# Latent attention: the products with the values one unit later and between the scores and the transposes

## The chip, the cores and the metric

The kernel runs on one core of one Trainium2 chip. The metric is the time of one execution on the device in microseconds (us), lower is better. TensorE is the matrix engine, ScalarE, VectorE and GpSimd (POOL in the profile) are the other compute engines, SyncE (SP) issues the DMAs.

## The reference

Two sequences of 1024 tokens, width 1024, go through two layers of an encoder. Every layer normalises x, projects it with `w_in` to the columns of four head groups, and mixes them: a short gated convolution (A), multi-head latent attention (B), a Conformer convolution (C) and windowed attention (D). The four results are gated, joined, multiplied by `w_out`, normalised and added to x. What the change touches is group B:

```python
def attend(args):
    qn_b, qr_b = args
    sc = (jnp.einsum('bqhd,bkhd->bhqk', qn_b, k_nope)
          + jnp.einsum('bqhr,bkr->bhqk', qr_b, k_rot)).astype(jnp.float32) * scale
    p = jax.nn.softmax(sc, axis=-1).astype(v.dtype)
    return jnp.einsum('bhqk,bkhd->bqhd', p, v)
```

There are 4 heads of 64 value columns, and a query has 64 + 32 rotary columns. Every query sees all 1024 keys.

## The kernel before, in words

The program makes four passes, one for each layer of each sequence. Each engine has its own instruction list, written out by hand in one block per engine, and runs it strictly in order; semaphores connect them. The numbers are fp32 split into a high and a low fp32r part, so that a product is three matmuls (high x high, high x low, low x high).

A pass is: input projection (L535, with the windowed attention worked into it), the latent up-projections (L696 to L720), the attention loop of group B, and the output product (L814). The attention loop works on **units**. A unit u is one head (u // 8) and one block of 128 queries (u % 8), 32 units in all (`NB`). Two units make a pair w = u // 2, whose 256 queries go through the products with the values together. A unit needs:

- **S(u)**, `b_scores`, TensorE L763: six matmuls of 512 columns, the scores of 128 queries against 1024 keys, into one of two pairs of PSUM banks. It waits until the exponential of unit u-2 has read that pair (`be_ok`).
- the **max** of each row, `b_max`, VectorE L1613, and the **exponential** with its sum, `b_exp`, ScalarE L1211, into `Pb`.
- **T(u)**, `b_transpose`, TensorE L778: eight transposes of 128x128, in two halves, into banks 4 and 5. It waits for the exponential of u (`be_ok`) and until VectorE is done with the same half of unit u-1 (`bpt_lo`).
- the **high part**, `b_hi`, ScalarE L1219, and the **low part**, `b_lo`, VectorE L1349, two instructions each, from PSUM into `PTb`.
- **V(u)**, `b_out`, TensorE L798: eight matmuls of 256 columns. V(2w) takes the first four blocks of 128 keys of pair w, V(2w+1) the other four. Both write columns 0 to 255 of bank 6 + w % 2. In front of V(2w) stands **R(w)**, TensorE L793, two transposes that spread the reciprocals of the sums over columns 256 to 511 of the same bank. R(w) waits for the reciprocals (`br_ok`), and until the combine of pair w-2 has read the bank (`bo_ok`). V(2w) then waits for all low parts of the pair.
- the **tmpB copy**, `b_half`, ScalarE L1230, and the **combine**, `b_combine`, VectorE L1634, L1635 and L1637: the two parts added, times gate, times reciprocal, into `cat`. The combine signals `bo_ok`.

The order is that of the loops over i, one on each engine. In step i TensorE issues S(i), T(i-1) and V(i-3). VectorE issues the max of i, the low parts of i-1, and in even steps from 6 on the combine of pair (i-6)/2 (with the reciprocals of a pair in between). ScalarE issues the high parts of i-1, the exponential of i, and in odd steps from 5 on the tmpB copy of pair (i-5)/2. ScalarE also does other work there: in steps 10, 11, 18 and 19 it copies keys and queries of the heads 2 and 3 (`HEAD_AT`), in steps 20, 22, 24, 26 and 28 it splits a block of `w_out` (`W_OUT_AT`, L1041), and in 27, 31 and 32 it splits columns of `cat` for the output product, whose first two blocks TensorE issues in step 33. The wait that R(w) makes, and the end of the combine, are these lines:

```python
if half == 0:
    if w >= 2:
        pe.wait_ge(*got("bo_ok", w - 1))
...
own.add(tt(b[rows, 0:256], b[rows, 0:256], t, ALU.add))
own.add(stt(y_, b[rows, 256:512], 0.5, y_, ALU.mult, ALU.mult))
own.wait()
tt(y_, b[rows, 0:256], y_, ALU.mult).then_inc(q["bo_ok"], 1)
```

Of the kernel before, what the change touches and what calls it, by code (L numbers as in the profile page):

```python
# [88 lines left out]
NB = HEADS * NT  # L89
# [34 lines left out]
def build(nc, x, w_in, w_out, w_q, w_kv, w_pw, par, g_pre, g_post, rel_bias, onehot, band, rope, y):  # L124
    with ExitStack() as ctx:
# [190 lines left out]
        def got(name, n, ahead=0):  # L316

            return q[name], (now[0] + ahead) * TOTAL[name] + n
# [60 lines left out]
        with nc.Block() as block:  # L379
# [128 lines left out]
            def _(pe):  # L508
                pe.wait_ge(p_id, 2)
                for p in range(PASSES):  # L510
# [218 lines left out]
                    def pointwise(m):  # L729
                        dst = (bank67, bank45)[m]  # L730
                        if m == 0:
                            pe.wait_ge(*got("clo_ok", 2))
                            pe.wait_ge(*got("bc_cp", 2))
                        else:
                            pe.wait_ge(*got("y_ok", 2))
                        for j in range(2):
                            for a, b in three:
                                z = (cHi, cLo)[b]
                                for h in range(2):
                                    last = mm(dst[:, h * HALF:(h + 1) * HALF], wpR[:, a, j, m * P:(m + 1) * P],  # L740
                                              z[:, j, h * HALF:(h + 1) * HALF],
                                              start=(j == 0 and (a, b) == (0, 0)),
                                              stop=(j == 1 and (a, b) == (1, 0)))
                        last.then_inc(q["pw_mm"], 1)
# [23 lines left out]
                    def b_transpose(u):  # L768

                        pe.wait_ge(*got("be_ok", u + 1))  # L770
                        for half in range(2):
                            if u >= 1:
                                pe.wait_ge(*got("bpt_lo", 2 * u + half - 1))
                            else:
                                pe.wait_ge(*got("pw_ok", 2))
                            for k in range(NT // 2):
                                col = half * HALF + k * P
                                last = tr(ps[:, 4 + half, k * P:(k + 1) * P], Pb[:, u % 2, col:col + P], ident[:, :])  # L778
                            last.then_inc(q["bt_mm"], 1)

                    def b_out(w, half):


                        h = 2 * w // NT
                        bank = ps[:, 6 + w % 2, :]
# [3 lines that stand above are left out]
                            elif w == 0:  # L789
                                pe.wait_ge(*got("pw_ok", 1))  # L790
                            pe.wait_ge(*got("br_ok", w + 1))
                            for i in range(2):
                                tr(bank[:, 256 + i * P:256 + (i + 1) * P],  # L793
                                   brc[:, 2 * w + i:2 * w + i + 1].broadcast_to([P, P]), ident[:, :])
                            pe.wait_ge(*got("bpt_lo", 4 * w + 4))
                        for k in range(half * NT // 2, (half + 1) * NT // 2):
                            for part in range(2):
                                last = mm(bank[:, 0:256], Vb[:, k, h, :, :], PTb[:, w % 2, part, k, :],  # L798
                                          start=(k == 0 and part == 0), stop=(k == NT - 1 and part == 1))
                        if half:  # L800
                            last.then_inc(q["bo_mm"], 1)
# [18 lines left out]

                    pe.wait_ge(*got("vb_lo", NT))
                    pointwise(0)
                    for i in range(NB + 3):
                        if i == 1:
                            pointwise(1)
                        if i < NB:
                            b_scores(i)
                        if 1 <= i < NB:
                            b_transpose(i - 1)
                        if i == NB + 1:  # L830
                            out_product(0, (0, 1))
                        if i >= 3:
                            b_out(*divmod(i - 3, 2))
                        if i == NB:
                            b_transpose(NB - 1)


                    out_product(0, range(2, KD))
# [136 lines left out]
            def _(act):  # L975
# [33 lines left out]
                for p in range(PASSES):  # L1009
# [192 lines left out]
                    def q_hi(h):  # L1202
                        Q, rows = ((Qe, slice(0, HD)), (Qo, slice(HD, P)))[h % 2]
                        act.wait_ge(*got("ch_done", C["bqn0"] + 1))
                        act.activation(Q[rows, 0, :], (chunk_ps("bqn0"), qF2)[h // 2][rows, :], ACT.Copy).then_inc(q["q_hi"], 1)
# [7 lines left out]
                    def b_hi(u):  # L1213
                        w = u // 2
                        if w >= 2:
                            act.wait_ge(*got("bo_mm", w - 1))
                        for half in range(2):
                            act.wait_ge(*got("bt_mm", 2 * u + half + 1))
                            act.activation(PTb[:, w % 2, 0, half * NT // 2:(half + 1) * NT // 2, u % 2 * P:(u % 2 + 1) * P],  # L1219
                                           ps[:, 4 + half, :].rearrange("p (k t) -> p k t", t=P), ACT.Copy  # L1220
                                           ).then_inc(q["bpt_hi"], 1)

                    def b_half(w):
                        h = 2 * w // NT
                        act.wait_ge(*got("bo_mm", w + 1))
                        if w >= 2:
                            act.wait_ge(*got("bo_ok", w - 1))
                        r, o = ((0, HD), (HD, 0))[h % 2]
                        b = ps[:, 6 + w % 2, :]
                        act.activation(tmpB[r:r + HD, w % 2, :], b[o:o + HD, 0:256], ACT.Copy).then_inc(q["bo_tmp"], 1)  # L1230
# [8 lines left out]
                    k_hi(1)  # L1239
                    q_hi(0)  # L1240
                    q_hi(1)
                    for i in range(NB + 4):
                        if i in HEAD_AT:
                            h = HEAD_AT[i]
                            (q_hi if i % 2 else k_hi)(h)
                        if 1 <= i <= NB:
                            b_hi(i - 1)
                        if i < NB:
                            b_exp(i)
                        if i >= 5 and i % 2 == 1:  # L1250
                            b_half((i - 5) // 2)
                        if i in W_OUT_AT:
                            split_hi(f"w_out{W_OUT_AT[i]}")
                        if i == CAT_A_AT:
                            act.wait_ge(*got("bs_mm", NB - NT))
                            cat_hi(0, slice(0, 2))
                        if i in (NB - 1, NB):
                            act.wait_ge(*got("bo_ok", NB // 2 - NT // 2 + 1))
                            cat_hi(i - NB + 1, slice(2, KD) if i < NB else slice(0, KD))
# [40 lines left out]
            def _(dve):  # L1300
# [41 lines left out]
                for p in range(PASSES):  # L1342
# [284 lines left out]
                    def b_combine(w):  # L1627
                        h, i = divmod(2 * w, NT)
                        dve.wait_ge(*got("bo_tmp", w + 1))
                        r = HD * (h % 2)  # L1630
                        rows = slice(r, r + HD)
                        b, t = ps[:, 6 + w % 2, :], tmpB[rows, w % 2, :]
                        y_ = cat[rows, 2 + h // 2, i * P:(i + 2) * P]
# [4 lines that stand above are left out]
# [7 lines left out]
                    k_lo(1)  # L1645
                    q_lo(0)
                    q_lo(1)
                    for i in range(NB + 5):
                        if i < NB:
                            b_max(i)  # L1650
                        if i == 0:
                            pointwise_gate(0)
                            pointwise_gate(1)
                        if 1 <= i <= NB:
                            if i % 2 == 0:
                                b_recip(i // 2 - 1)
                            b_lo(i - 1)
                        if i >= 6 and i % 2 == 0:
                            b_combine((i - 6) // 2)

                    for k in range(EARLY, KD):
                        split_lo(f"w_out{k}")
# [136 lines left out]
```

## Time and profile before

| what | value |
|---|---|
| median of 3 runs | 2217.1 us (2217.02 to 2217.55) |
| profiled execution, its own time | 2217.08 us |
| profiled execution, span from first to last instruction | 2215.2 us |
| granted TensorE clock, mean | 0.999 |
| busy: TensorE matmuls, weight loads, VectorE, ScalarE, GpSimd | 98%, 83%, 73%, 44%, 25% |

In the profile PE is TensorE, PEld its weight loads, DVE VectorE, ACT ScalarE and POOL GpSimd. A row of the timeline names its start, how long the merged instructions took, the engine, the source line, what is written and read, and how many instructions it merges; the number in brackets is the engine's idle time in front of it and who ended it. Matmuls overlap in their pipeline: the duration of a group runs past the start of the next group, so the step from start to start is the time it occupies.

### The profile page before, as it was taken

What the parts mean: (1) busy time and instruction counts of PE and PEld (TensorE: products, weight loads), DVE (VectorE), ACT (ScalarE), POOL (GpSimd) and SP (SyncE); (2) the same over time, 40 slices, a digit from 0 to 9 for tenths busy, and PEclk for the clock granted to TensorE, in tenths of its full rate; (3) what the DMA queues carried; (4) which work ended last, traced back from release to release, by engine and by line L of the source; (5) the groups of instructions that cost most, each with busy time, mean ns of one, the idle gap of its engine ahead of it and who ended that gap; (6) DMA issues with size and microseconds to landing.
All of it is one profiled execution on the core that took longest, in us unless ns stands there. A gap on an engine that the chain in (4) does not pass through costs nothing.

```text
span 2215.2 us, 29044 instructions
## 1 busy us (share of the span) xinstructions
PE 2178.0 (98%) x11394; PEld 1834.1 (83%) x11394; DVE 1616.2 (73%) x2050; ACT 982.5 (44%) x1731; POOL 545.4 (25%) x316
## 2 busy tenths in 40 slices
PE   7999999999999999999999999999999999999998
PEld 7888887888888888788888888878888888887887
DVE  5499877975459987896455998789654699878853
ACT  4333335863333433585333343368533334337841
POOL 2122223221122232232111233223211212323310
PEclk9999999999999999999999999999999999999999
DMA  5111111034111111103311111100432111110012
GB/s 182 58 39 52 31 42 49 10 113 146 67 66 39 43 39 43 39 19 146 113 61 63 39 43 39 53 29 23 154 111 76 39 48 43 39 43 29 30 67 95
DMA packets 38951, 136.34 MB, mean 62 GB/s; under 512 B 4736, under 2 KB 5248, under 8 KB 38816
## 3 DMA queue, kind: packets, MB, share of 16 engines
q1 hardware_dynamic: 38816, 134.47, 18.0%
q8 instruction: 93, 1.52, 0.3%
q14 instruction: 42, 0.34, 0.1%
HBM read 116.63 MB, written 17.83 MB: 61 GB/s over the span
## 4 chain that ended last, share of the span: by engine, by line
PE 91%; DVE 5%; ACT 2%; issue 1%; DMA 0%; SPq 0%; DVEq 0%; ACTq 0%
PE ps L535 48%; PE ps L814 14%; PE ps L763 7%; PE ps L798 5%; PE ps L778 5%; PE ps L640 2%; PE ps L614 2%; PE ps L628 2%; DVE accC L1430 2%; PE ps L696 1%; PE ps L283 1%; PE ps L740 1%; PE ps L545 1%; DVE woR L1349 1%; PE ps L793 1%
## 5 line engine op out<-in xcount | busy, mean ns | idle before, releaser
L535 PE MATMUL ps<-hT,stat 128*128 128x512 f32 x4416 | 1055.1, 393 | 0.8 <-DVE Qst L1349 0.8
L535 PEld LDWEIGHTS ps<-hT,stat 128*128 128x128 f32 x4416 | 816.6, 188 | 164.1 <-issue 2.9
L890 POOL TENSOR_TENSOR stat<-raw,stat 128x1024 fp32r<-128x1024 f32 x92 | 250.1, 2719 | 871.2 <-ACT stat L1041 871.2
L1430 DVE SCALAR_TENSOR_TENSOR accC<-uC,parT,accC 128x1024 f32<-128x1024 f32 x240 | 421.4, 1793 | 2.6
L814 PE MATMUL ps<-woR,catR 128*128 128x512 f32 x1488 | 343.7, 391 | 3.4 <-DVE woR L1349 3.4
L814 PEld LDWEIGHTS ps<-woR,catR 128*128 128x128 f32 x1488 | 277.6, 188 | 61.9 <-DVE woR L1349 5.1
L1613 DVE TENSOR_REDUCE bnb<-ps 128x1 f32<-128x1024 f32 x128 | 156.2, 1220 | 43.1 <-PE ps L763 42.4
L1219 ACT ACTIVATE PTb<-ps 128x512 fp32r<-128x512 f32 x256 | 139.0, 595 | 81.0 <-PE ps L778 78.8
L1349 DVE TENSOR_TENSOR PTb<-ps,PTb 128x512 fp32r<-128x512 f32 x256 | 163.4, 679 | 12.8 <-ACT PTb L1219 11.9
L1211 ACT ACTIVATE Pb<-ps,bnb 128x1024 f32<-128x1024 f32 x128 | 143.0, 1118 | 21.0 <-DVE bnb L1613 20.0
L798 PE MATMUL ps<-PTb,Vb 128*128 128x256 f32 x1024 | 151.4, 292 | 0.0
L778 PEld LDWEIGHTS ps<-ident,Pb 128*128 128x128 f32 x1024 | 117.7, 140 | 28.1 <-ACT Pb L1211 13.2
L778 PE MATMUL ps<-ident,Pb 128*128 128x128 f32 x1024 | 133.7, 273 | 5.5 <-ACT Pb L1211 5.0
L1289 ACT ACTIVATE junk<-ps 128x1024 f32<-128x1024 f32 x31 | 31.8, 1027 | 236.7 <-PE ps L814 236.7
L1108 ACT ACTIVATE PTd<-ps 128x768 fp32r<-128x768 f32 (+1 forms) x64 | 48.6, 759 | 189.5 <-PE ps L628 189.5
L798 PEld LDWEIGHTS ps<-PTb,Vb 128*128 128x128 f32 x1024 | 129.5, 190 | 0.0
L1693 DVE TENSOR_SCALAR oss<-oss 128x1 f32<-128x1 f32 x31 | 4.8, 154 | 156.5 <-ACT junk L1289 134.8
L1115 ACT ACTIVATE tmpD<-ps 64x128 f32<-64x128 f32 x64 | 17.5, 273 | 207.4 <-PE ps L640 207.4
L1047 ACT ACTIVATE th<-ps 128x1024 f32<-128x1024 f32 x40 | 41.1, 1027 | 144.0 <-PE ps L535 144.0
L763 PE MATMUL ps<-Ke,Qe 96*128 96x512 f32 x384 | 100.1, 396 | 0.0
L1453 DVE CUSTOM_DVE_ANT_0 Pd<-ps,bias,ngs 128x384 f32<-128x384 f32 (+1 forms) x128 | 67.2, 563 | 44.8 <-PE ps L614 44.8
L763 PE MATMUL ps<-Ko,Qo 128*128 128x512 f32 x384 | 99.6, 394 | 0.0
(201 smaller groups left out, 2809.9 us busy)
## 6 DMA issues: line engine op xcount, KB each, us to landing
raw<-w_in SPq DMA_DIRECT2D x100, 512.0 KB, 3.5
y<-xs SPq DMA_DIRECT2D x31, 512.0 KB, 2.6
raw<-w_out SPq DMA_DIRECT2D x24, 512.0 KB, 3.6
xs<-x SPq DMA_DIRECT2D x16, 512.0 KB, 3.6
xs<-y SPq DMA_DIRECT2D x16, 512.0 KB, 3.5
xd<-x SPq DMA_DIRECT2D x8, 512.0 KB, 9.0
ropeT<-rope SPq DMA_DIRECT2D x4, 1024.0 KB, 5.7
rawX<-w_out SPq DMA_DIRECT2D x8, 512.0 KB, 4.2
```

What stands on the lines that cost most here:

```text
L535: last = mm(ps[:, 2 * (c % 2) + h, cols], w[:, a, k, :], hT[:, h, b, k, cols], start=(k == 0 and (a, b) == (0, 0)), stop=(k == KD - 1 and ...
L763: last = mm(pair(u + 1)[:, half * HALF:(half + 1) * HALF], Q[0:rows, a, i * P:(i + 1) * P], Kk[0:rows, b, half * HALF:(half + 1) * HALF], ...
L778: last = tr(ps[:, 4 + half, k * P:(k + 1) * P], Pb[:, u % 2, col:col + P], ident[:, :])
L798: last = mm(bank[:, 0:256], Vb[:, k, h, :, :], PTb[:, w % 2, part, k, :], start=(k == 0 and part == 0), stop=(k == NT - 1 and part == 1))
L814: last = mm(ps[:, 2 * (n % 2) + h, :], catR[:, n % 2, a, k, :], woR[k][:, b, h * HALF:(h + 1) * HALF], start=(k == 0 and (a, b) == (0, 0)) ...
L890: pool.tensor_tensor(dst[:, 1], src, dst[:, 0].bitcast(F32), ALU.subtract).then_inc(q["wlo"], 1)
L1211: act.activation(Pb[:, u % 2, :], pair(u + 1), ACT.Exp, bias=bnb[:, u:u + 1], accum_out=bsm[:, u:u + 1]).then_inc(q["be_ok"], 1)
L1219: act.activation(PTb[:, w % 2, 0, half * NT // 2:(half + 1) * NT // 2, u % 2 * P:(u % 2 + 1) * P], ps[:, 4 + half, :].rearrange("p (k t) - ...
L1349: return tt(dst, a, hi.bitcast(F32), ALU.subtract)
L1430: last_tap[j] = conv.add(stt(accC[:, j, :], uC[:, j, t:t + T], w, accC[:, j, :], ALU.mult, ALU.add))
L1453: last = dve.tensor_tensor_reduce(out=Pd[:, g, 0:nk * P], in0=ps[:, 4 + g, 0:nk * P], in1=bias[:, h, b0:b0 + nk * P], scale=-D_SCALE, scal ...
L1613: dve.tensor_reduce(bnb[:, u:u + 1], pair(u + 1), AX.X, ALU.max, negate=True).then_inc(q["bm_ok"], 1)
```

## The change

TensorE's loop gets one more step. In step i it now issues S(i), then V(i-4), then T(i-1), where it was S(i), T(i-1), V(i-3). ScalarE's tmpB copy moves from odd steps (i-5)/2 to even steps (i-6)/2, and VectorE's combine from even steps (i-6)/2 to odd steps (i-7)/2. At the end V(29) comes behind T(31) and in front of the first blocks of the output product, V(30) and V(31) behind them.

```diff
-                    for i in range(NB + 3):
+                    for i in range(NB + 4):
                         if i == 1:
                             pointwise(1)
                         if i < NB:
                             b_scores(i)
-                        if 1 <= i < NB:
+                        if i >= 4:
+                            b_out(*divmod(i - 4, 2))
+                        if 1 <= i <= NB:
                             b_transpose(i - 1)
                         if i == NB + 1:
                             out_product(0, (0, 1))
-                        if i >= 3:
-                            b_out(*divmod(i - 3, 2))
-                        if i == NB:
-                            b_transpose(NB - 1)
...
-                    for i in range(NB + 4):
+                    for i in range(NB + 5):
...
-                        if i >= 5 and i % 2 == 1:
-                            b_half((i - 5) // 2)
+                        if i >= 6 and i % 2 == 0:
+                            b_half((i - 6) // 2)
...
-                    for i in range(NB + 5):
+                    for i in range(NB + 6):
...
-                        if i >= 6 and i % 2 == 0:
-                            b_combine((i - 6) // 2)
+                        if i >= 7 and i % 2 == 1:
+                            b_combine((i - 7) // 2)
```

TensorE's list before, around R(3): T(7), V(5), S(9), T(8), R(3) and V(6). A wait stands behind the instruction that makes it.

```order
L778 MATMUL ps<-ident,Pb 128x128 [waits bpt_lo,be_ok]
L778 MATMUL ps<-ident,Pb 128x128 x3
L778 MATMUL ps<-ident,Pb 128x128 [waits bpt_lo]
L778 MATMUL ps<-ident,Pb 128x128 x3
L793 MATMUL ps<-ident,brc 128x128 [waits br_ok,bo_ok]
L793 MATMUL ps<-ident,brc 128x128
L798 MATMUL ps<-PTb,Vb 128x256 [waits bpt_lo]
L798 MATMUL ps<-PTb,Vb 128x256 x7
L763 MATMUL ps<-Ko,Qo 128x512 [waits be_ok]
L763 MATMUL ps<-Ko,Qo 128x512 x5
```

The change, the same place: T(8), S(10), R(3) and V(6).

```order
L778 MATMUL ps<-ident,Pb 128x128 [waits bpt_lo,be_ok]
L778 MATMUL ps<-ident,Pb 128x128 x3
L778 MATMUL ps<-ident,Pb 128x128 [waits bpt_lo]
L778 MATMUL ps<-ident,Pb 128x128 x3
L763 MATMUL ps<-Ko,Qo 128x512 [waits be_ok]
L763 MATMUL ps<-Ko,Qo 128x512 x5
L793 MATMUL ps<-ident,brc 128x128 [waits br_ok,bo_ok]
L793 MATMUL ps<-ident,brc 128x128
L798 MATMUL ps<-PTb,Vb 128x256 [waits bpt_lo]
L798 MATMUL ps<-PTb,Vb 128x256 x7
```

S(10) moved from behind V(6) to in front of R(3), and still stands behind T(8).

VectorE's list before, around the combine of pair 1: max(8), the reciprocals of pair 3, the low parts of T(7), the combine of pair 1 and max(9).

```order
L1613 TENSOR_REDUCE bnb<-ps 128x1 [waits bs_mm]
L1625 RECIPROCAL brc<-bsm 128x2 [waits be_ok]
L1349 TENSOR_TENSOR PTb<-ps,PTb 128x4x128 [waits bpt_hi] x2
L1634 TENSOR_TENSOR ps<-ps,tmpB 64x256 [waits bo_tmp]
L1635 SCALAR_TENSOR_TENSOR cat<-ps,cat 64x256
L1637 TENSOR_TENSOR cat<-ps,cat 64x256 [waits own_dve]
L1613 TENSOR_REDUCE bnb<-ps 128x1 [waits bs_mm]
```

The change, with all lines two lower in number: max(8), reciprocals, low parts of T(7), max(9), low parts of T(8), the combine of pair 1, max(10).

```order
L1611 TENSOR_REDUCE bnb<-ps 128x1 [waits bs_mm]
L1623 RECIPROCAL brc<-bsm 128x2 [waits be_ok]
L1347 TENSOR_TENSOR PTb<-ps,PTb 128x4x128 [waits bpt_hi] x2
L1611 TENSOR_REDUCE bnb<-ps 128x1 [waits bs_mm]
L1347 TENSOR_TENSOR PTb<-ps,PTb 128x4x128 [waits bpt_hi] x2
L1632 TENSOR_TENSOR ps<-ps,tmpB 64x256 [waits bo_tmp]
L1633 SCALAR_TENSOR_TENSOR cat<-ps,cat 64x256
L1635 TENSOR_TENSOR cat<-ps,cat 64x256 [waits own_dve]
L1611 TENSOR_REDUCE bnb<-ps 128x1 [waits bs_mm]
```

The combine of pair 1, which releases R(3), moved from behind the low parts of T(7) to behind those of T(8).

## Rows read from the trace of the kernel before

**Rows 1.** The page: busy time; then all waits of TensorE: line, releaser, us, times, longest.

```profile
PE 2178.0 (98%) x11394; PEld 1834.1 (83%) x11394; DVE 1616.2 (73%) x2050; ACT 982.5 (44%) x1731; POOL 545.4 (25%) x316
...
PE ps L793 <- DVE cat L1637: 2.5, 4, 0.6
```

**Rows 2.** The first attention loop: us, busy (instructions) of each engine, clock, DMA share, GB/s.

```profile
363.90:479.70 115.80, 113.81 (x762) 100.53 (x760) 99.53 (x160) 87.43 (x155) 32.00 (x16) 1.00 0.11 37
```

**Rows 3.** Timeline of TensorE, units 7 to 10: start, us, engine, line, operation, count.

```profile
392.25 1.04 PE L778 MATMUL ps<-ident,Pb 128*128 128x128 f32 x8
393.04 1.20 PE L798 MATMUL ps<-PTb,Vb 128*128 128x256 f32 x8
394.08 1.55 PE L763 MATMUL ps<-Ko,Qo 128*128 128x512 f32 x6
395.47 1.03 PE L778 MATMUL ps<-ident,Pb 128*128 128x128 f32 x8
396.34 0.38 PE L793 MATMUL ps<-ident,brc 128*128 128x128 f32 x2
396.48 1.20 PE L798 MATMUL ps<-PTb,Vb 128*128 128x256 f32 x8
397.52 1.55 PE L763 MATMUL ps<-Ko,Qo 128*128 128x512 f32 x6
```

**Rows 4.** The same view: S(18), T(18), V(28) with V(29), T(31), R(15).

```profile
427.55 1.55 PE L763 MATMUL ps<-Ke,Qe 96*128 96x512 f32 x6
429.43 1.09 PE L778 MATMUL ps<-ident,Pb 128*128 128x128 f32 x8 [0.33 <-ACT Pb L1211]
...
470.74 2.15 PE L798 MATMUL ps<-PTb,Vb 128*128 128x256 f32 x16
473.05 1.09 PE L778 MATMUL ps<-ident,Pb 128*128 128x128 f32 x8
...
477.52 0.43 PE L793 MATMUL ps<-ident,brc 128*128 128x128 f32 x2 [0.62 <-DVE cat L1637]
```

**Rows 5.** Timelines of three engines: T(1), its high parts, low parts, the next max.

```profile
372.51 1.09 PE L778 MATMUL ps<-ident,Pb 128*128 128x128 f32 x8 [0.43 <-ACT Pb L1211]
373.20 1.08 ACT L1219 ACTIVATE PTb<-ps 128x512 fp32r<-128x512 f32 x2 [0.75 <-PE ps L778]
373.83 1.29 DVE L1349 TENSOR_TENSOR PTb<-ps,PTb 128x512 fp32r<-128x512 f32 x2 [0.42 <-ACT PTb L1219]
375.04 1.22 DVE L1613 TENSOR_REDUCE bnb<-ps 128x1 f32<-128x1024 f32 x1
```

**Rows 6.** Timelines: combine of pair 0 and of pair 4, and R(6) on TensorE.

```profile
388.18 0.42 DVE L1634 TENSOR_TENSOR ps<-ps,tmpB 64x256 f32<-64x256 f32 x1
388.51 0.41 DVE L1635 SCALAR_TENSOR_TENSOR cat<-ps,cat 64x256 f32<-64x256 f32 x1
388.96 0.42 DVE L1637 TENSOR_TENSOR cat<-ps,cat 64x256 f32<-64x256 f32 x1
...
414.95 0.44 DVE L1634 TENSOR_TENSOR ps<-ps,tmpB 64x256 f32<-64x256 f32 x1
...
415.88 0.43 DVE L1637 TENSOR_TENSOR cat<-ps,cat 64x256 f32<-64x256 f32 x1
...
416.37 0.43 PE L793 MATMUL ps<-ident,brc 128*128 128x128 f32 x2
```

**Rows 7.** Timeline of ScalarE: tmpB copy, head copy, high parts of T(9); a w_out split.

```profile
398.43 0.38 ACT L1230 ACTIVATE tmpB<-ps 64x256 f32<-64x256 f32 x1
398.71 1.04 ACT L1200 ACTIVATE Ke<-kF 64x1024 fp32r<-64x1024 f32 x1
399.78 1.09 ACT L1219 ACTIVATE PTb<-ps 128x512 fp32r<-128x512 f32 x2
...
449.20 1.07 ACT L1041 ACTIVATE woR<-raw 128x1024 fp32r<-128x1024 f32 x1
```

**Rows 8.** Windows of TensorE: us, busy (instructions), granted clock, DMA share, GB/s.

```profile
15.00:18.00 3.00, 2.68 (x16) 0.71 1.02 402
1446.00:1452.00 6.00, 4.34 (x23) 1.00 0.01 1
```

## The prediction, made before the changed kernel ran

> **What bounds the kernel now.** The busy shares come first: TensorE's matmuls fill 98% of the span, no other engine 75% [rows 1]. So TensorE's own instruction order sets the end, and an edit that removes none of its work can give back only idle time, or add some. The stage is read next: the attention loop lies at 363.9 to about 480 us in the first of four passes, and in those 115.8 us TensorE is busy 113.8 at a granted clock of 1.00, which is the level of 2.4 GHz [rows 2]. The other three passes repeat it within 0.2 us. Then the timeline of one pair of units, from T(7) to S(10): every group starts where the one before lets it. Start to start, scores (S, six matmuls) take 1.39 us, transposes (T, eight) 0.79, products with the values (V, eight) 1.04, the two transposes of the reciprocals (R, in front of every even V) 0.14, with 0.08 more between T and R [rows 3]. A pair takes 6.66 us, and no wait stands in these rows. So the idle time left is at the loop's edges: 0.4 us twice while the pipeline fills (one of them in [rows 5]), 0.5 at unit 18, 0.2 before T(31), 0.6 before R(15) [rows 4].
>
> **What the order asks for.** Two things are asked of the other engines. T(u) needs the exponential of unit u. In the old order T(u) follows its own S(u) after T(u-1), V and S(u+1). In the new one another V stands in between, 1.04 us more slack. R(w) needs the combine of pair w-2, because it writes the PSUM bank that this combine reads (b_out waits on bo_ok of w-2). VectorE issues the combine in program order, behind the max and the two low-part subtractions of its step.
>
> Before, the combine of pair w stands behind the subtractions of unit 2w+5 and R(w+2) comes behind T(2w+6). So two groups, V and S(2w+7), and then T(2w+6) lie between T(2w+5) and R(w+2). Now the combine stands behind the subtractions of unit 2w+6, and R(w+2) comes behind S(2w+8): a single group lies between T(2w+6), on which the combine now hangs, and R(w+2). That is the term that decides.
>
> **The chain, step by step,** from the start of T(2w+6), call it t.
> - ScalarE's copy of the high parts starts 0.69 us after T. VectorE's subtraction starts 0.63 us after the copy, and the next VectorE instruction 1.21 us after the subtraction [rows 5]. So the combine starts at t + 2.53.
> - Its three instructions take 1.20 us for even heads (from 388.18 to 389.38) and 1.36 for odd ones (from 414.95 to 416.31) [rows 6]. TensorE starts 0.06 us after such an end, as the row of R at 416.37 shows [rows 6]. So R can start at t + 3.79, or t + 3.95.
> - TensorE itself is ready for R at t + 0.79 + 1.39 = t + 2.18 [rows 3].
>
> The stall is 1.61 us, or 1.77 for odd heads. It does not get shorter from pair to pair. R stands in TensorE's queue in front of V, the next T and the next S, and the next even T, which starts the next such chain, is behind them. VectorE is no escape: it finished max(2w+7) before, at about t + 0.4, since S(2w+7) ends 1.04 us before t.
>
> The wait exists for w = 2 to 14, 13 times in a pass. For R(15) it is gone, since V(29) and two blocks of the output product stand between T(31) and it.
>
> **Additions.** At i = 10, 18 and 11, 19 ScalarE copies the keys and queries of a late head, and at i = 20, 22, 24, 26, 28 it splits a block of w_out. The steps of T(2w+6) that meet one are those of i = 11, 19 and the five even i. In the old order tmpB copy and head copy stood in this sequence once: from T(8) at 395.47 to the next high-part copy at 399.78 it took 4.31 us. The next T now stands 3.22 us after the last (0.79 + 1.39 + 1.04), and its copy is wanted 0.69 after that: 0.40 late, twice [rows 3, 7]. The w_out split takes as long (1.07 us against 1.04) and now also stands behind a tmpB copy, which it did not before; its start at 449.20 overlaps the read of the accumulator a little, so I choose 0.35 late, five times [rows 7]. R(14) is different: step 32 has no scores, so the stall is bare of the 1.39 us that covered it, 3.00 instead of 1.61. Odd heads' combines (numbers 4 to 7 and 12) add 0.16 five times.
>
> Sum of stalls in a pass: 12 x 1.61 + 3.00 + 5 x 0.16 + 2 x 0.40 + 5 x 0.35 = 25.7 us.
>
> **What goes away.** The 0.08 us between T and R, 15 times (1.2 us): behind S, whose matmuls are long enough to hide a weight load, as they do before T. A further 0.3, where the combines of odd heads already held R back a little (the one that ends at 416.31 by the row of R(6) at 416.37). T(18) started 1.88 us behind its S instead of 1.39 [rows 4]: 0.5. T(31), due 2 x 1.04 us behind the start of V(28), came after 2.3, and R(15) waited 0.62: 0.2 and 0.6 [rows 4]. Together 2.8 us. The two waits of the fill stay, as no V stands in steps 2 and 3 in either order. The wait for w_out6 behind the loop stays too: its chain starts at the end of V(31).
>
> **Costed at nothing.** The extra V in flight needs no buffer. The high-part copy of unit 2w waits for V(2w-3), which now stands right in front of T(2w), so it is done. The max of the next unit stands behind the late combine: it ends at about t + 4.9 and its exponential by 6.2, while the transposes that need it come at 3.79 + 0.14 + 1.04 + 0.79 + 1.39 + 1.04 = t + 8.2. The tail keeps V(30) and V(31) side by side behind the output product. No DMA issue is moved, and no instruction of SyncE or POOL.
>
> Net per pass: 25.7 - 2.8 = 22.9 us; four passes 91.6. The profiled execution took 2217.08 us (span 2215.2), the median of the runs is 2217.1, so both give **2309 us**, 4.1% slower.
>
> **A rule against the sum.** VectorE's subtraction pair issues its next instruction 1.21 us after it starts, for two instructions of 0.68, and the combine's first two are 0.33 us apart though the first lasts 0.42 [rows 5, 6]. So neighbours overlap.
> The Trainium skill (VectorE: DVE Perf Modes, section The DRAIN you can't avoid) says that after each operation a flush of about its duration less 266 ns must pass before the next starts. By that, an estimate, the subtractions would take 2 x (0.68 + 0.41) and the combine 3 x (0.42 + 0.15), about 1.4 us more in each of the 13 stalls, and the time would be 2382 us.
> The rows are of the very instructions in question, so the sum goes by them. In this case's rows such a gap is not seen.
>
> **Bounds.** Low: 13 stalls of 1.61, no additions, all savings: 13 x 1.61 - 2.8 = 18.1 a pass, 2289.6 us. High: odd-head combine and a late copy everywhere, R(14) at 3.56, and only half of the savings: 12 x 2.17 + 3.56 - 1.4 = 28.2 a pass, 2330 us.
>
> **Rivals.**
> 1. The new slack wins and the combine is not late (4 in 100). Then only the savings show: 2217.1 - 4 x 2.8 = **2206 us**, faster. For it: the exponential is the wait the rows name at T, and it gets 1.04 us of room. Against it: the chain above is longer than S by 1.61 us, each link from a row; it turns only if the combine needs less than 2.18 us from T. A half-way case, stalls of about 0.2 us that eat the savings, leaves no change (1 in 100).
> 2. The clock falls (3 in 100). TensorE would stand still about 1.6 to 2.0 us in every 8.3. Near the start, between 15 and 18 us, the granted clock was 0.71, a mixture of the levels of 2.4 and 1.2 GHz. Against it, between 1446 and 1452 us TensorE was busy only 4.34 of 6 us, and the clock stayed 1.00 [rows 8]. At 0.71 throughout the loop, 115.8 us would become 163, and the time 2309 + 4 x 47 = about **2500 us**.
> The Trainium skill (TensorE: Matmul & The Clock Gate, section A second HAM failure mode: psum-queue depth-cycling) describes a kernel in which frequent short idles between groups of matmuls made the clock go up and down. By that rule the loop would run at mixed levels, as in this rival. The window at 1446 us speaks against it.
> 3. The flush as above, 2382 us (1 in 100).
> 4. The change does not do what it says: the rows of the order show that it does; no chance is kept.
>
> **How the numbers follow.** The forecast has 91 in 100: 2309, and its bounds 2289 to 2330 are the range, with about 6 in 100 left inside the forecast for values beyond them, and the 9 of the others outside. A measurement here can tell 0.2%, 4.4 us. Faster: 0.04. Same: 0.01. Slower: 0.95.
>
> **What would show it.** In the changed profile: TensorE waits at the first reciprocal transpose (L793) for VectorE's last combine instruction, some 13 to 14 times a pass and 1.6 to 2.2 us each, about 3 once, in all near 100 us for that line (before: 2.5 in the whole run [rows 1]). A pair takes 8.2 us instead of 6.66. The waits at T for the exponential shrink to the fill's two. The granted clock stays 1.00. The loop ends about 23 us later in every pass, and the parts outside keep their length. I am wrong if that line shows no wait, if waits are much above 2.2 us, or if the clock of the loop's windows drops.

## The result: 5.2% slower, and the profile after

The changed kernel takes 2334.1 us (2332.4 to 2335.5, 4 runs) against 2217.2 us, a ratio of 1.052 with an interval of 1.051 to 1.054. The forecast was 2309 us with a range up to 2330: the direction and the wait came as said, the time is 25 us above the forecast and 4 us above the range. Ratios are of undisturbed runs: of the ten runs of the version with the combine put back, one took 2411.9 us at a clock of 0.85 and does not enter its ratio.

The page's busy times; the span grew from 2215.2 to 2331.2 us, TensorE's busy time only from 2178.0 to 2208.0 [rows 1]:

```profile
PE 2208.0 (95%) x11394; PEld 1857.4 (80%) x11394; DVE 1621.3 (70%) x2050; ACT 980.7 (42%) x1731; POOL 544.4 (23%) x316
```

The waits of TensorE, us in total, times, longest:

```profile
PE ps L793 <- DVE cat L1635: 91.1, 52, 3.0
```

R waited 2.5 us in the whole run [rows 1], and now 91.1 us, in 52 waits. That is 13 in each of four passes, the number the prediction gave.

The timeline of TensorE with T(6), S(8), R(2) and T(8) answers to [rows 3]:

```profile
388.81 1.04 PE L778 MATMUL ps<-ident,Pb 128*128 128x128 f32 x8
389.60 1.63 PE L763 MATMUL ps<-Ko,Qo 128*128 128x512 f32 x6
392.59 0.43 PE L793 MATMUL ps<-ident,brc 128*128 128x128 f32 x2 [1.35 <-DVE cat L1635]
...
397.01 1.04 PE L778 MATMUL ps<-ident,Pb 128*128 128x128 f32 x8
```

From S(8) to R(2) it now takes 2.99 us, with 1.35 of standstill. A pair takes 8.20 us (388.81 to 397.01) instead of 6.66. ScalarE's and VectorE's rows of the same stretch show the chain, from T(6) at 388.81:

```profile
389.51 1.09 ACT L1217 ACTIVATE PTb<-ps 128x512 fp32r<-128x512 f32 x2 [0.63 <-PE ps L778]
...
390.14 1.29 DVE L1347 TENSOR_TENSOR PTb<-ps,PTb 128x512 fp32r<-128x512 f32 x2 [0.80 <-ACT PTb L1217]
391.35 0.41 DVE L1632 TENSOR_TENSOR ps<-ps,tmpB 64x256 f32<-64x256 f32 x1
...
392.12 0.42 DVE L1635 TENSOR_TENSOR cat<-ps,cat 64x256 f32<-64x256 f32 x1
```

The high parts start 0.70 us after T, the low parts at 1.33, the combine (L1632 to L1635) at 2.54, its end stands at 3.73 and R at 3.78. The prediction had 0.69, 1.32, 2.53, 3.73 and 3.79. The step without scores, T(30) and R(14):

```profile
495.48 1.04 PE L778 MATMUL ps<-ident,Pb 128*128 128x128 f32 x8
499.55 0.43 PE L793 MATMUL ps<-ident,brc 128*128 128x128 f32 x2 [3.03 <-DVE cat L1635]
```

What the prediction did not have shows in the next rows. The first two are R(6) and, 3.48 us later, V(13). The others are R(7), V(14), T(17), S(19) and V(15), one pair later. Both R stand behind a standstill of 1.65 us:

```profile
426.06 0.43 PE L793 MATMUL ps<-ident,brc 128*128 128x128 f32 x2 [1.65 <-DVE cat L1635]
...
429.54 1.12 PE L798 MATMUL ps<-PTb,Vb 128*128 128x256 f32 x8
...
434.57 0.43 PE L793 MATMUL ps<-ident,brc 128*128 128x128 f32 x2 [1.65 <-DVE cat L1635]
434.75 1.77 PE L798 MATMUL ps<-PTb,Vb 128*128 128x256 f32 x8
436.33 1.91 PE L778 MATMUL ps<-ident,Pb 128*128 128x128 f32 x8
437.89 1.92 PE L763 MATMUL ps<-Ke,Qe 96*128 96x512 f32 x6
439.65 1.12 PE L798 MATMUL ps<-PTb,Vb 128*128 128x256 f32 x8
```

V(14) lasts 1.77 us instead of 1.20, and T takes 1.56 from start to start instead of 0.79. From R(7) to V(15) it takes 5.08 us, 1.6 more than from R(6) to V(13). A group V longer than 1.20 us stands right behind R(7), R(8), R(9) and R(14) in this pass, and four, three and four times in the other passes, 15 times in all. The windows show why: us, busy and count, granted clock, DMA share, GB/s, of the four loops and of these few microseconds:

```profile
363.90:509.00 145.10, 121.51 (x761) 0.95 0.09 30
940.00:1087.00 147.00, 123.05 (x770) 0.95 0.10 33
1517.00:1664.00 147.00, 123.53 (x777) 0.97 0.10 33
2093.00:2240.00 147.00, 123.27 (x769) 0.95 0.10 33
434.50:439.00 4.50, 4.43 (x22) 0.62 0.01 2
```

Inside the stretch from 434.5 to 439 the granted clock is 0.62, so much of it ran at the level of 1.2 GHz. Over the loops it is 0.95 to 0.97, where the loop before had 1.00 [rows 2]. The loop, from S(0) to the third block of the output product, took 115.8 us in every pass before, and takes 145.1, 145.1, 143.5 and 145.3 now (363.95 to 509.07 in the first); the 143.5 is the pass with three long V. Their growth adds up to 115.9 of the 116.0 us that the span grew.

### The profile page after: what moved, and what is told of

Its sections match the earlier page's. It is cut to its first block, busy times and chain, and to the rows that moved or that the text cites. A ratio compares the mean times of both kernels' runs of the same rounds, so it can differ in the third digit from the quotient of the medians.

```text
span 2331.2 us, 29044 instructions
## 1 busy us (share of the span) xinstructions
PE 2208.0 (95%) x11394; PEld 1857.4 (80%) x11394; DVE 1621.3 (70%) x2050; ACT 980.7 (42%) x1731; POOL 544.4 (23%) x316
## 4 chain that ended last, share of the span: by engine, by line
PE 85%; DVE 9%; ACT 4%; issue 1%; DMA 0%; SPq 0%; ACTq 0%; DVEq 0%
PE ps L535 45%; PE ps L814 14%; PE ps L798 5%; PE ps L778 4%; PE ps L763 4%; DVE PTb L1347 3%; PE ps L640 2%; PE ps L614 2%; ACT PTb L1217 2%; PE ps L628 2%; DVE accC L1428 1%; PE ps L696 1%; PE ps L793 1%; PE ps L283 1%; DVE cat L1635 1%; PE ps L740 1%
## 5 line engine op out<-in xcount | busy, mean ns | idle before, releaser
L798 PE MATMUL ps<-PTb,Vb 128*128 128x256 f32 x1024 | 159.3, 302 | 0.0
L798 PEld LDWEIGHTS ps<-PTb,Vb 128*128 128x128 f32 x1024 | 144.4, 204 | 4.7
L778 PE MATMUL ps<-ident,Pb 128*128 128x128 f32 x1024 | 144.2, 288 | 3.6 <-ACT Pb L1209 3.5
L778 PEld LDWEIGHTS ps<-ident,Pb 128*128 128x128 f32 x1024 | 124.9, 149 | 8.7 <-ACT Pb L1209 7.0
L793 PE MATMUL ps<-ident,brc 128*128 128x128 f32 x128 | 28.7, 308 | 91.1 <-DVE cat L1635 91.1
L763 PE MATMUL ps<-Ke,Qe 96*128 96x512 f32 x384 | 105.1, 409 | 0.0
L793 PEld LDWEIGHTS ps<-ident,brc 128*128 128x128 f32 x128 | 13.7, 141 | 114.2 <-DVE cat L1635 112.6
L763 PE MATMUL ps<-Ko,Qo 128*128 128x512 f32 x384 | 104.4, 407 | 0.0
```

The source lines that it names most:

```text
L763: last = mm(pair(u + 1)[:, half * HALF:(half + 1) * HALF], Q[0:rows, a, i * P:(i + 1) * P], Kk[0:rows, b, half * HALF:(half + 1) * HALF], ...
L793: tr(bank[:, 256 + i * P:256 + (i + 1) * P], brc[:, 2 * w + i:2 * w + i + 1].broadcast_to([P, P]), ident[:, :])
```

## The experiments

Two questions were open. Is it the place of the combine that costs, or TensorE's new order as such? And are the 25 us that the sum missed the clock's fall, and is it the standstills that cause it?

**The combine and the tmpB copy back where they were**, with TensorE's new order:

```diff
-                        if i >= 6 and i % 2 == 0:
-                            b_half((i - 6) // 2)
+                        if i >= 5 and i % 2 == 1:
+                            b_half((i - 5) // 2)
...
-                        if i >= 7 and i % 2 == 1:
-                            b_combine((i - 7) // 2)
+                        if i >= 6 and i % 2 == 0:
+                            b_combine((i - 6) // 2)
```

> The changed kernel, with the tmpB copy on ScalarE and the combine on VectorE put back to the steps they had before (tmpB of pair w in step 2w+5, combine in step 2w+6); TensorE keeps its new order. Theory (the combine is late): the combine then hangs on T(2w+5), so the 52 waits of R vanish, the clock stays at 0.999, and the new order's savings show: about 2209 us (2203 to 2218). Rival (the new order on TensorE costs time by itself, by what stands next to what or by the clock): still above 2300 us.

Measured: 2215.8 us, ratio to the kernel before 0.9993 (0.9983 to 1.0002), clock 0.999. TensorE's timeline at S(8) and R(2), and T(31) at the loop's end:

```profile
389.94 1.63 PE L763 MATMUL ps<-Ko,Qo 128*128 128x512 f32 x6
391.40 0.38 PE L793 MATMUL ps<-ident,brc 128*128 128x128 f32 x2
...
472.86 1.09 PE L778 MATMUL ps<-ident,Pb 128*128 128x128 f32 x8 [1.11 <-ACT Pb L1209]
```

No wait at R: 1.46 us behind S. All of the 117 us are gone although TensorE's order is the new one, so the order as such costs nothing once the combine is not late. The savings were smaller than the 8 us expected: T(31) now waits 1.11 us in each pass, and a pair still takes 6.65 us (385.93 to 392.58). Against the kernel before, the gain of 1.4 us cannot be told from none.

**The combine in its late step, but in front of the low parts:**

```diff
                         if i < NB:
                             b_max(i)
...
+                        if i >= 7 and i % 2 == 1:
+                            b_combine((i - 7) // 2)
                         if 1 <= i <= NB:
                             if i % 2 == 0:
                                 b_recip(i // 2 - 1)
                             b_lo(i - 1)
-                        if i >= 7 and i % 2 == 1:
-                            b_combine((i - 7) // 2)
```

> The changed kernel, with the combine still in odd steps 2w+7 but between the max and the two low-part subtractions instead of behind them. Theory: only the two subtractions (and the copy they wait for) make the combine late, so this is as good as putting it back: no waits at R but a short one of 0.9 us at R(14), clock 0.999, about 2209 us (2203 to 2220). Rival (the step is what counts, the combine one unit later is too late wherever it stands in it): waits of over 1 us remain at R and the time stays above 2270 us.

Measured: 2213.2 us (2212.6 to 2214.6), ratio 0.9983 (0.9974 to 0.9992). VectorE's timeline, max(7), combine of pair 0, low parts of T(6):

```profile
388.21 1.21 DVE L1611 TENSOR_REDUCE bnb<-ps 128x1 f32<-128x1024 f32 x1
389.34 0.41 DVE L1632 TENSOR_TENSOR ps<-ps,tmpB 64x256 f32<-64x256 f32 x1
...
390.11 0.42 DVE L1635 TENSOR_TENSOR cat<-ps,cat 64x256 f32<-64x256 f32 x1
390.46 1.27 DVE L1347 TENSOR_TENSOR PTb<-ps,PTb 128x512 fp32r<-128x512 f32 x2
```

and TensorE's waits:

```profile
PE ps L793 <- DVE cat L1635: 3.8, 4, 1.0
PE ps L778 <- ACT Pb L1209: 3.5, 8, 0.4
```

The combine ends at 390.53. T(6) stands at 388.89 and R at 391.15 there, so it is 0.6 us early, and the four waits left are those of R(14). So it is not the step that was late, but its place behind two subtractions that hang on the last T. This version is ahead of both kernels, of the one before by 4 us, at the edge of what can be told.

**Three more matmuls in the wait.** They write into the PSUM pair that the next scores overwrite, and nothing reads them:

```diff
+                            if 2 <= w <= 13:
+                                u = 2 * w + 5
+                                Q, Kk, rows = ((Qe, Ke, NOPE + ROPE), (Qo, Ko, P))[((u - 1) // NT) % 2]
+                                pe.wait_ge(*got("be_ok", u - 1))
+                                for _ in range(3):
+                                    mm(pair(u + 1)[:, 0:HALF], Q[0:rows, 0, 0:P], Kk[0:rows, 0, 0:HALF],
+                                       start=True, stop=True)
                             if w >= 2:
                                 pe.wait_ge(*got("bo_ok", w - 1))
```

> The changed kernel, with three more matmuls of 512 columns in front of the wait of R(w), w = 2 to 13, into the pair of PSUM banks that the next scores overwrite; their results are not used. They wait for the exponential that frees the pair, so the standstill of 1.5 us and more is cut into about 0.7 us and a short rest, and the combine is as late as before. Theory (the 25 us beyond the sum of the stalls are the clock's fall after long standstills): the granted clock is back near 0.999 and the time falls to about 2311 us (2305 to 2318). Rival A (the clock falls for another reason, such as the transposes): clock stays 0.989 and time 2334. Rival B (the fillers are not free, since VectorE or ScalarE are slowed or R comes behind them): 2334 to 2345 us.

Measured: 2317.2 us, 17 us faster than the changed kernel although it does more. S(8), the three matmuls and R(2), and the windows of the same four stretches as above:

```profile
389.79 1.63 PE L763 MATMUL ps<-Ko,Qo 128*128 128x512 f32 x6
391.93 0.96 PE L792 MATMUL ps<-Ko,Qo 128*128 128x512 f32 x3 [0.51 <-ACT Pb L1216]
392.77 0.43 PE L800 MATMUL ps<-ident,brc 128*128 128x128 f32 x2
```

```profile
363.90:509.00 145.10, 131.72 (x822) 1.00 0.09 31
940.00:1087.00 147.00, 133.01 (x820) 0.99 0.08 26
1517.00:1664.00 147.00, 133.11 (x817) 0.99 0.11 34
2093.00:2240.00 147.00, 133.26 (x815) 0.99 0.08 26
```

R still comes 3.77 us behind T(6) (389.00 here), so the chain is as long as before, but TensorE stands still 0.51 us at a time there, and the granted clock of the loops is 0.99 to 1.00. So the clock comes back although the combine is as late as before. The three matmuls both shorten the standstill and add work to it, and this run does not tell which of the two counts. Three falls are left in the loops, one in each pass after the first: those loops take 140.7 to 140.9 us, where the first, which has none, takes 139.4. That is about 4 of the 6 us above the expected 2311. The rest fits R(8), R(9) and R(10), which come up to 0.3 us later than in the changed kernel, since the added matmuls wait up to 1.3 us for a late exponential (R(8) stands 4.66 us behind T(18), where it was 4.37).

**The late combine alone**, in the kernel before:

```diff
-                        if i >= 6 and i % 2 == 0:
-                            b_combine((i - 6) // 2)
+                        if i >= 7 and i % 2 == 1:
+                            b_combine((i - 7) // 2)
```

> The kernel before, with one part of the change alone: VectorE's combine in odd steps (i - 7) / 2. TensorE's order and the tmpB copies are as before. Theory: R(w+2) now stands directly behind T(2w+6), with no scores in between, so R waits until 3.78 us after that T's start instead of 0.87, 2.9 us for each of 13 pairs, 38 us a pass: 2217 + 152 = 2369 us at full clock, and up to 2420 with the clock's falls after so long standstills. Rival (the late combine costs the same 1.6 us wherever R stands): about 2305 us.

Measured: 2434.3 us, ratio 1.098, clock 0.967, and 150.3 us of waits at R. T(6), then R(2) and R(3), each with the V behind it:

```profile
390.33 1.04 PE L778 MATMUL ps<-ident,Pb 128*128 128x128 f32 x8
394.11 0.69 PE L793 MATMUL ps<-ident,brc 128*128 128x128 f32 x2 [2.74 <-DVE cat L1637]
394.45 2.06 PE L798 MATMUL ps<-PTb,Vb 128*128 128x256 f32 x8
...
405.02 0.43 PE L793 MATMUL ps<-ident,brc 128*128 128x128 f32 x2 [2.75 <-DVE cat L1637]
405.21 1.20 PE L798 MATMUL ps<-PTb,Vb 128*128 128x256 f32 x8
```

R stands 3.78 us behind T(6), as expected: the same chain, with nothing in between. The 2369 us at full clock was a sum of such waits, and the waits came out as summed (147.8 us more than before, where 152 had been expected). The 65 us on top are more than the 50 that I allowed for the clock, so the time lies 14 us above the range. The rows also show that not every standstill lets the clock fall: after the one of 2.74 us at 394.11 V lasts 2.06 us, after the one of 2.75 at 405.02 it lasts 1.20.

**TensorE's order alone**, without the extra unit, in the kernel before:

```diff
-                        if 1 <= i < NB:
-                            b_transpose(i - 1)
-                        if i == NB + 1:
-                            out_product(0, (0, 1))
-                        if i >= 3:
-                            b_out(*divmod(i - 3, 2))
-                        if i == NB:
-                            b_transpose(NB - 1)
+                        if 3 <= i < NB + 1:
+                            b_out(*divmod(i - 3, 2))
+                        if 1 <= i <= NB:
+                            b_transpose(i - 1)
+                        if i == NB + 1:
+                            out_product(0, (0, 1))
+                        if i >= NB + 1:
+                            b_out(*divmod(i - 3, 2))
```

> The kernel before, with TensorE's order alone changed: S(i), V(i-3), T(i-1), no extra unit of distance; ScalarE and VectorE as before. Theory (what counts is how many groups stand between the T on which the combine hangs and R): here T(2w+5) and R(w+2) have only S(2w+7) between them, as T(2w+6) and R(w+2) have in the changed kernel, so the same waits of 1.4 to 2.0 us come back at R, 13 a pass and a longer one at R(15), 25 us a pass: 2317 us at full clock, 2317 to 2345 with the clock's falls. Rival (the lateness comes from the extra unit alone): no waits at R, 2210 to 2225 us.

Measured: 2318.0 us, ratio 1.045, clock 0.995. T(5), S(7) and R(2):

```profile
387.14 1.04 PE L778 MATMUL ps<-ident,Pb 128*128 128x128 f32 x8
387.94 1.63 PE L763 MATMUL ps<-Ke,Qe 96*128 96x512 f32 x6
390.92 0.43 PE L793 MATMUL ps<-ident,brc 128*128 128x128 f32 x2 [1.35 <-DVE cat L1637]
```

R comes 3.78 us behind T(5), with only S(7) between. So neither the late step nor the extra unit is needed to make the combine late; the rule of the prediction, one group between the T it hangs on and R, holds in another arrangement. That the time meets the expected 2317 us is in part luck. The 25 us a pass were for full clock, and the clock of the four loops was 0.98 or 0.99. The first loop is 24.9 us longer than before (140.65 against 115.79), but it holds two falls, of about 1.6 us each: V behind R(7) and R(8) lasts 1.49 and 1.39 us instead of 1.20. So the stalls came out about 3 us a pass lower than expected, and the falls made up for part of it.

**The extra unit and the late steps, in the old order:**

```diff
-                        if i >= 4:
-                            b_out(*divmod(i - 4, 2))
                         if 1 <= i <= NB:
                             b_transpose(i - 1)
+                        if i >= 4:
+                            b_out(*divmod(i - 4, 2))
```

> The changed kernel with TensorE's old order in a step: S(i), T(i-1), V(i-4), so that of the change the extra unit and the later steps of tmpB copy and combine are left. R(w+2) has T(2w+7) in front of it and is no longer late (3.97 us behind the start of T(2w+6) against 3.78 needed). But VectorE's max of the next even unit stands behind the combine, and T has no V in front of it: I expect waits of about 1.0 us at every odd T for its exponential instead, 13 a pass, and 3.3 at R(14): 17 us a pass, 2286 us (2270 to 2300), clock near 0.999. Rival (once R is not late nothing is): 2212 to 2222 us.

Measured: 2288.1 us, ratio 1.032, clock 0.997. T(6), V(3), S(8), T(7) and R(2), ScalarE's high parts of T(6) with the exponential of unit 7, and the wait's sum:

```profile
391.43 1.04 PE L778 MATMUL ps<-ident,Pb 128*128 128x128 f32 x8
392.23 1.20 PE L798 MATMUL ps<-PTb,Vb 128*128 128x256 f32 x8
393.27 1.55 PE L763 MATMUL ps<-Ko,Qo 128*128 128x512 f32 x6
395.70 1.09 PE L778 MATMUL ps<-ident,Pb 128*128 128x128 f32 x8 [0.89 <-ACT Pb L1209]
396.63 0.38 PE L793 MATMUL ps<-ident,brc 128*128 128x128 f32 x2
...
393.47 1.09 ACT L1217 ACTIVATE PTb<-ps 128x512 fp32r<-128x512 f32 x2 [2.19 <-PE ps L798]
394.44 1.12 ACT L1209 ACTIVATE Pb<-ps,bnb 128x1024 f32<-128x1024 f32 x1
```

```profile
PE ps L778 <- ACT Pb L1209: 61.1, 68, 2.3
```

As expected R is free and T(odd) waits 0.89 us instead, for its exponential, and the time is about 2 us from the 2286 expected. But the cause that was expected is not the one that shows, so the time was met by luck. The max of unit 7 ends at 392.86 on VectorE, and the combine of pair 0, the first of all, starts only at 395.30. T(5) at 387.93 already waits the same 0.89 us, before there is any combine. What is late is ScalarE's copy of the high parts of T(6): it stands still for 2.19 us and starts when V(3) ends, because it writes the half of `PTb` that V(3) reads (`b_hi` waits for V(2w-3)). The exponential of unit 7 stands behind that copy in ScalarE's list, and T(7) waits for it. ScalarE waits for V in this way 56 times in this run, 14 a pass; no such wait shows in the changed kernel.

The wait of 3.3 us expected at R(14) did not come either; T(31), in front of it, waits 2.27 us. The first loop is 17.8 us longer than before in all (133.55 against 115.79). The prediction costed the buffer at nothing, since V(2w-3) stands right in front of T(2w) in the changed kernel. This run shows that this holds only by TensorE's new order: with the extra unit and the old order the same buffer costs a wait a pair.

**The splits of w_out in odd steps:**

```diff
-W_OUT_AT = {NB * 5 // 8 + 2 * k: k for k in range(EARLY)}
+W_OUT_AT = {NB * 5 // 8 + 1 + 2 * k: k for k in range(EARLY)}
```

> The changed kernel, with ScalarE's five splits of w_out moved from the steps 20, 22, 24, 26, 28 to 21, 23, 25, 27, 29. Theory: they then stand ahead of high parts of odd units, which the combine does not hang on, so five waits a pass fall from about 1.7 to 2.0 us to 1.4 to 1.65: 6.6 us in all, and the clock falls after some of them go too (up to 10 us): about 2321 us (2313 to 2329). Rival (the splits do not matter to the chain): 2334 us, waits unchanged.

Measured: 2321.0 us (2317.4 to 2325.4), clock 0.993 in the profiled run. R(8), R(11) and R(13) of the first pass:

```profile
442.85 0.43 PE L793 MATMUL ps<-ident,brc 128*128 128x128 f32 x2 [2.24 <-DVE cat L1635]
...
469.52 0.43 PE L793 MATMUL ps<-ident,brc 128*128 128x128 f32 x2 [1.36 <-DVE cat L1635]
...
485.94 0.43 PE L793 MATMUL ps<-ident,brc 128*128 128x128 f32 x2 [1.35 <-DVE cat L1635]
```

R(11) to R(13) waited 1.69 to 1.70 us in the changed kernel and 1.35 or 1.36 here, so ScalarE's splits were in the chain as costed. R(8), whose term is the head copy, keeps its longer wait. The profiled run is 15.6 us shorter than that of the changed kernel (2317.4 against 2333.0), and the waits at R give 5.7 of it (85.4 us against 91.1); the clock, 0.993 against 0.989, fits the rest, about 10 us. It also differs from run to run: 0.989 in the one of 2325.4 us.

## Why the forecast was right in kind and 25 us short

**The chain: right.** For even heads every link came out within 0.02 us, and there were 13 waits in every pass. For odd heads R(6) came 4.07 us behind T(14) where 3.95 had been worked out: the combine starts 1.32 us behind the subtractions there (423.31 to 424.63), not 1.21. From the rows of the first pass, R(2) to R(13) come 21.6 us in all later than their normal 1.47 us behind S, and R(14) 3.3 us later than the 0.79 behind T. That is 24.8 us a pass; the prediction summed 25.7, counting from 1.39.

**The additions: right.** The late heads' copies, the splits and the odd heads' longer combines were costed at 3.35 us a pass, and come to 3.6 in the first. R(4) came 4.14 us behind T(10) (405.21 to 409.35) where 4.19 had been worked out. The splits alone are shown by their experiment.

**What goes away: too high by about 1.2 us a pass.** The 0.08 us between T and R did not vanish "behind S". It moved: S takes 1.46 to 1.47 us before a V or R, in place of 1.39 before a T. In the version with the combine back in place a pair takes 6.65 us, as against 6.66. This and the 0.9 us by which the stalls came out lower nearly cancel: (24.8 - 1.6) x 4 = 92.8, where 91.6 was forecast.

**The clock: the step that failed.** The prediction took "The granted clock stays 1.00", so its sum has nothing for the clock, and gave its fall 3 chances in 100 as a rival that holds all through the loop, for 2500 us. What came is between the two: three or four falls in each pass, each for a few microseconds around the end of a standstill. The rows of R(7) put one at 1.6 us, so the 15 cost about 24 us, and 117 - 92.8 = 24 were missing. The loops' mean clock of 0.95 to 0.97 over 145 us says the same, 4 to 7 us a pass. The prediction had itself named a drop of the loops' clock as a sign of being wrong. The row I argued from, 4.34 busy of 6 us at full clock [rows 8], was one stretch with one wait of 1.3 us and one of 0.4; it said nothing on standstills of 1.65 to 3.0 us that come back every 8 us. The range had no term for a partial fall and ended at 2330. With a term for a clock of 0.95 over 145 us a pass, 29 us, its upper end would have stood at 2359. The rule that the prediction took from the Trainium skill (TensorE: Matmul & The Clock Gate, A second HAM failure mode: psum-queue depth-cycling), that short standstills between groups make the clock go up and down, agrees with this trace: 0.62 in the stretch at 434.5 us, 0.95 over the loop.

**The rule on VectorE's flush** (the Trainium skill, VectorE: DVE Perf Modes, The DRAIN you can't avoid) would by the prediction's estimate have added 1.4 us to each stall (its own terms add up to 1.5). R stood 3.78 us behind T, not 5.2: in this trace it does not lengthen such a chain. The prediction left out that the same section limits the rule: a next operation that is not held starts earlier.

**The rivals.** That the new slack for the exponential wins was wrong in the changed kernel, and right once the combine is moved: the waits of T for it fell from 5.0 to 3.5 us, and the version with the combine before the low parts gains 4 us on the kernel before. The forecast of 2.8 us a pass for it was too high for the reason above.

## What to carry to other kernels

When work is moved on one engine, measure in groups how far each wait's releaser is ahead of it, and not only for the wait that the move is meant to relax: here T gained 1.04 us of slack, and R lost two of the three groups that stood between it and the T that its combine hangs on. Before, 4.1 us lay between them (T(7) to R(3) [rows 3]), now 2.2, and the chain needs 3.8. Where an engine runs in order, the place inside a step can cost as much as the step: the combine behind two subtractions cost 117 us, in front of them nothing. A term that costs nothing in one order can cost a wait in another, as the buffer of the high parts did when TensorE kept its old order. And a standstill of TensorE near 2 us that comes back in a loop should be priced with a partial fall of its clock on top of its own length.

## What the runs showed of the hardware that was not expected

The clock's fall is not a matter of one standstill's length. In the changed kernel standstills of 1.65 us were followed by full speed at 426.06 and by the lower level at 434.57, and four later ones of 1.69 or 1.70 us, R(10) to R(13), by full speed. With the late combine alone, some of 2.7 us were followed by full speed and others not. What the engine did before those that differ is nearly the same in the rows, and what decides between them stays open; no run here was made for it.
